# Recurrence scores in column tiles: blocks of 32 keys by 32 queries in place of whole 128 by 128 products

## The reference, cut to what matters

```python
def _hgrn2_scan(q, k, v, log_f, s0):
    """Chunkwise S_t = diag(f_t) S_{t-1} + k_t v_t^T, o_t = S_t^T q_t."""
    def step(S, xs):
        qc, kc, vc, lfc = xs
        b = jnp.cumsum(lfc, axis=1)
        b_last = b[:, -1]
        o_inter = jnp.einsum('bthk,bhkv->bthv', qc * jnp.exp(b), S)
        decay = jnp.exp(jnp.where(tri, b[:, :, None] - b[:, None, :], -jnp.inf))
        scores = jnp.einsum('bthk,btshk,bshk->bhts', qc, decay, kc)
        o_intra = jnp.einsum('bhts,bshv->bthv', scores, vc)
```

## Time and profile before

| what | value |
|---|---|
| runs, median (lowest to highest) | 2563.21 us (2562.05 to 2564.33), 3 runs |
| profiled execution, its own time | 2560.08 us |
| its span, first to last instruction | 2558.3 us |
| mean granted PE clock | 0.992 |
| PE busy | 2489.7 us (97%), 13364 matmul records |
| PEld busy | 1947.6 us (76%), 13364 weight loads |
| DVE busy | 1195.6 us (47%) |
| ACT busy | 604.2 us (24%) |
| POOL busy | 269.0 us (11%) |
| level scores, line 831, on PE | 120.5 us in 896 records |
| diagonal, line 828, on PE | 16.1 us in 128 records |
| DMA, mean over the span | 111 GB/s |

### The profile page before, as it was taken

One profiled execution on the slowest core, in us unless ns is written; L12 is line 12 of the kernel. 1 busy time (PEld: TensorE's weight loads), 2 busy tenths in 40 slices (PEclk: granted clock), 3 DMA queues, 4 the chain that ended last, 5 costly groups with the idle time before them and its releaser, 6 DMA issues.

```text
span 2558.3 us, 32946 instructions
## 1 busy us (share of the span) xinstructions
PE 2489.7 (97%) x13364; PEld 1947.6 (76%) x13364; DVE 1195.6 (47%) x2007; ACT 604.2 (24%) x1205; POOL 269.0 (11%) x194
## 2 busy tenths in 40 slices
PE   7999999999999898999999999999999999999999
PEld 3688888888887577867885444788885687889998
DVE  3176696696786613343234111256663014116961
ACT  3123233232332113143224000121211023113211
POOL 0011211122121000000000000112120000003410
PEclk9999999999999999999999999999999999999999
DMA  9443343443334042410520222233243132354662
GB/s 357 165 171 139 118 148 116 142 169 115 131 110 137 26 131 82 132 50 23 142 66 1 66 66 90 82 90 85 83 111 85 51 83 66 113 175 124 173 178 63
DMA packets 320673, 284.88 MB, mean 111 GB/s; under 512 B 27137, under 2 KB 300169, under 8 KB 320057
## 3 DMA queue, kind: packets, MB, share of 16 engines
q1 hardware_dynamic: 318810, 279.08, 35.4%
q0 software_dynamic: 1280, 4.20, 0.5%
q10 hardware_dynamic: 479, 0.13, 0.0%
HBM read 280.24 MB, written 3.15 MB: 111 GB/s over the span
## 4 chain that ended last, share of the span: by engine, by line
PE 79%; DVE 13%; issue 3%; ACT 2%; DMA 1%; SPq 0%; DVEq 0%; ACTq 0%
PE ps L1454 11%; PE ps L1383 10%; PE ps L733 7%; PE ps L1533 5%; PE ps L793 4%; PE ps L1521 4%; PE ps L1421 3%; PE ps L1395 3%; PE ps L784 2%; PE ps L917 2%; PE ps L935 2%; PE ps L1012 2%; PE ps L831 2%; DVE arena L2451 2%; DVE arena L2090 2%
## 5 line engine op out<-in xcount | busy, mean ns | idle before, releaser
L1383 PE MATMUL ps<-hT,ring_mem 128*128 128x512 f32 (+1 forms) x768 | 250.3, 486 | 0.0
L1383 PEld LDWEIGHTS ps<-hT,ring_mem 128*128 128x128 f32 x768 | 145.9, 190 | 101.3 <-issue 91.4
L2382 DVE TENSOR_TENSOR arena<-ps,arena 128x512 f32<-128x512 f32 (+1 forms) x48 | 26.8, 558 | 291.3 <-PE ps L1395 291.3
L733 PE MATMUL ps<-xT,ring_mem 128*128 128x256 f32 x672 | 159.8, 381 | 1.6 <-DVE ring_mem L2134 1.4
L733 PE MATMUL ps<-hT,ring_mem 128*128 128x256 f32 x672 | 158.8, 379 | 0.0
L733 PEld LDWEIGHTS ps<-xT,ring_mem 128*128 128x128 f32 x672 | 126.7, 190 | 22.8 <-issue 3.8
L733 PEld LDWEIGHTS ps<-hT,ring_mem 128*128 128x128 f32 x672 | 126.1, 190 | 18.9 <-issue 2.9
L1454 PE MATMUL ps<-hT,arena 128*128 128x256 f32 (+1 forms) x704 | 131.6, 331 | 6.9 <-ACT hT L512 6.9
L831 PE MATMUL ps<-arena,K_c 128*128 128x128 f32 x896 | 120.5, 289 | 11.8 <-ACT K_c L1717 11.7
L831 PEld LDWEIGHTS ps<-arena,K_c 128*128 128x128 f32 x896 | 116.9, 195 | 18.9 <-ACT K_c L1717 11.5
L1454 PE MATMUL ps<-arena 128*128 128x256 f32 (+1 forms) x704 | 129.6, 327 | 0.0
(11 more groups left out here) (316 smaller groups left out, 4302.5 us busy)
## 6 DMA issues: line engine op xcount, KB each, us to landing
ring_mem<-in_w_mod_dram SPq DMA_DIRECT2D x24, 2048.0 KB, 7.7
ring_mem<-in_w_up_dram SPq DMA_DIRECT2D x88, 512.0 KB, 5.2
ring_mem<-in_hg_w_in_dram SPq DMA_DIRECT2D x40, 1024.0 KB, 5.2
ring_mem<-in_w_in_dram SPq DMA_DIRECT2D x30, 1024.0 KB, 5.4
ring_mem<-in_w_down_dram SPq DMA_DIRECT2D x16, 1408.0 KB, 7.0
ring_mem<-in_ada_w_dram SPq DMA_DIRECT2D x8, 2048.0 KB, 7.7
ring_mem<-in_mla_w_in_dram SPq DMA_DIRECT2D x9, 1024.0 KB, 5.5
ring_mem<-in_hg_w_out_dram SPq DMA_DIRECT2D x8, 1024.0 KB, 12.2
```

The lines of the kernel that those rows point to most:

```text
L733: mm = PE.matmul(dst, left[:, k, :], right[:, k, :], start=k == 0, stop=k == 3)
L1383: mm = PE.matmul(ps[:, j, 0:n], wj[:, k, m * 128:m * 128 + 128], hT[:, k, c0:T], start=k == 0, stop=k == 7)
```

## The change

Each product of 128 keys by 128 queries is replaced by products over tiles on the diagonal of the unit, each with its own columns of the array and its own PSUM partitions. For the diagonal and levels 1 to 6 (h up to 32) a tile has 32 keys and 32 queries, four to a unit. For h below 32 the queries are those of the same 32 tokens; at h = 32 they are those of the neighbouring 32 (`c ^ h`), all from one direction's buffer. Level 7 (h = 64) takes two tiles of 64 keys by 64 queries. What else stands in the two banks is not written any more, and the masks do not select it. Nothing is changed on DVE, ACT, POOL or in the DMAs.

```diff
--- before.py
+++ after.py
@@ -819,16 +819,24 @@
                     pe.wait_ge(rt_ready, raised(i * 2))
             else:
                 pe.wait_ge(kc_ready, i * LEVELS + term)
+            h = 1 << term >> 1
+            w_ = 64 if h == 64 else 32
             for b in range(2):
                 if term:
                     pe.wait_ge(lv_free, i * 16 + 2 * term + b - 1)
                 for u in range(4 * b, 4 * b + 4):
-                    dst = ps[:, LV[b], (u % 4) * 128:(u % 4) * 128 + 128]
-                    if term == 0:
-                        mm = PE.matmul(dst, k_sum[:, u * 128:u * 128 + 128], q_st[:, u * 128:u * 128 + 128], start=True, stop=True)
-                    else:
-
-                        mm = PE.matmul(dst, K_c[:, u * 128:u * 128 + 128], comb(Qw, 1 << (term - 1), u), start=True, stop=True)
+                    for c in range(0, 128, w_):
+
+                        if term == 0:
+                            q0, queries = c, q_st[:, u * 128 + c:u * 128 + c + w_]
+                        elif h < w_:
+                            q0, queries = c, view(Qw, (2 * h, w_ // (2 * h)), (PC + h, 2), (1, h), at=u * 128 + c)
+                        else:
+                            q0 = c ^ h
+                            at_ = u * 128 + q0 + (PC if q0 & h else 0)
+                            queries = Qw[:, at_:at_ + w_]
+                        keys = (K_c if term else k_sum)[:, u * 128 + c:u * 128 + c + w_]
+                        mm = PE.matmul(ps[c:c + w_, LV[b], (u % 4) * 128 + q0:(u % 4) * 128 + q0 + w_], keys, queries, start=True, stop=True)
                 mm.then_inc(lv_full, 1)
 
         def hg_turn_tensor(pe, i):
```

## The result

The changed kernel takes **2576.31 us** in the median (2572.26 to 2578.66, 5 runs) beside 2563.21 (2560.6 to 2564.33, 5 runs) of the kernel before: a ratio of 1.0053 (95% interval 1.0038 to 1.0067), some 13 us slower. The forecast of 2546 had the wrong sign, and the result lies above its range.

The account below looks back on a forecast made before the run. Scores on PE bound the first turn; middle turns run mostly through DVE, and DVE waits for scores in the tail. Gains 7.5 + 9.6 + 3.6 less 4 for fetches are 16.7 us: 2546 us median, range 2537 to 2561.

Parts of the forecast that it names:

- the fetch at the returns: At the loop's five returns: fetching the longer body costs 0.8 us each, 4 us, mostly hidden behind the mean products.
- rival (4): Last recurrence: PE idles more, its clock falls for two more stretches, some 5 us longer, 2551 us; chance 0.05.
- rival (1): Loop returns: the body no longer stays in PE's instruction memory, 2.5 us a return, 2555 us, at the bound 2562; chance 0.18.
- A block: 0.75 us: One score term on PE, 128 instructions near 6 ns each: 0.75 us where it took 1.78.
- rivals (2) and (3): PE's blocks: narrow matmuls queue, 2554 us, chance 0.10; or instruction supply lags, 40 ns a pair, 2606 us, chance 0.12.
- Level 7: 1.2 us: Level 7's block in two tiles takes about 1.2 us instead of 1.88, giving 0.7 us a middle turn.
- First turn: 7.5: First turn of the loop: 8.1 us less on PE, all on the chain, of which 7.5 reach the end.
- Level 1: 0.9 a turn: Middle turns: faster level 1 scores give DVE its 0.69 us wait and the 0.21 ahead of line 2150.
- Levels 2 to 6: nothing, beside DVE's chain: Middle turns: levels 2 to 6 are off the chain; their 4 us become waits of PE and gain nothing.
- Last recurrence: 3.6: Last recurrence: DVE's three waits for scores, 1.94, 0.57 and 1.14 us, can all go, 3.6 us.
- PE's new idle time in a middle turn: PE newly idles ahead of levels 3 to 6 and line 733, ended by ACT's K_c and DVE's lines 2142 and 2191.
- the signs listed: Wrong if a block takes over 1.8 us, a middle turn over 99.9 us, or PE's clock in the turns is below 1.00.

Follow-up runs that it names:

- e1: The changed kernel with PE's six looped turns written out, so PE never branches back: 2543.23 us, ratio 0.9929 to the kernel before.
- e3: The changed kernel with levels 5 and 6 in whole products inside the loop, a body of 1834 instructions: 2574.4 us, ratio 1.0044.
- e4: The changed kernel with levels 4 to 6 in whole products inside the loop, a body of 1738 instructions: 2573.18 us, ratio 1.0041.
- e7: The kernel before, without tiles, line 733's products in the loop done in two halves of 128 columns, 1770 instructions: 2591.33 us, ratio 1.0116.
- e14: The changed kernel, levels 3 to 6 whole in the loop (1642 instructions), first looped turn written out with all but level 6 in tiles: 2565.05 us.
- e6: The changed kernel with levels 3 to 6 in whole products inside the loop, a body of 1642 instructions: 2545.85 us, ratio 0.994.
- e12: The changed kernel, levels 4 to 6 whole in the loop (1738 instructions), first looped turn written out ahead, in tiles throughout: 2543.86 us, ratio 0.9925.
- e5: The changed kernel, first looped turn written out, only levels 1 and 7 in tiles in the five remaining looped turns (1450 instructions): 2538.35 us.
- e9: The changed kernel with every turn written out for PE, levels 1 and 7 alone in tiles in turns 3 to 7: 2536.92 us, ratio 0.9904.
- e13: The changed kernel, levels 3 to 6 whole in the loop (1642 instructions), first looped turn written out, in tiles throughout: 2544.17 us, ratio 0.9931.
- e2: The kernel before, without tiles, its six looped turns written out for PE as a control: 2560.79 us, ratio 0.9993.

## Why the prediction was wrong

**The term that failed is the fetch at the returns**: "I take 0.8 us a return, 4 us, taking most of a fetch to lie behind the two mean products". Measured are 31 us for five returns by the turns of e1 and the changed kernel (523.3 − 492.5), 6.2 each; the rows of e3, e4, e7 and e14 have the same wait. Three things were off.

- What was priced as one transfer is more. The branch takes 4.2 to 4.5 us, over five times 0.8, and above even the upper bound of 3.9.
- Hardly any of it lies behind the mean products. They end 1.98 us after the start of the last group, and PE still stands for 3.55: of a branch of 4.25 us only some 0.7 is covered, since the sequencer comes to it while they run and no sooner.
- The clock falls in the gap. The first eight records lose 1.5 us by it, and where the stretch at 1.2 GHz is 6.8 us long instead of 3.4, the turn has 105.2 to 105.6 us instead of 104.1 to 104.2. e14 shows the share of it: without the fall a return costs 3.7 to 3.8 us. This was in rival (4) only for the last recurrence, never as what a wait of rival (1) would bring with it.

So rival (1) was the right mechanism, at 0.18, and its price of 2.5 us, bound 3.9, was too low: at 6.2 the prediction's own sum gives 2546 − 4 + 31 = 2573, 3 us from the result. The sentence from the Trainium skill ("Runtime: NRT & Kernel Launch", section "Instruction fetch mechanics") gives the 2048 instructions in blocks of 256, from which the prediction itself worked out that each return would miss. The page's own warning is of a branch out of a window of two blocks. Taken so, 1322 instructions would wait as well, and the runs decide against it: up to 1738 return in 0.2 us. A memory of 2048 instructions with one block being fetched leaves seven blocks, and with that reading e4, e6, e12 and e14 agree. I set that reading against a wish, that PE would have work queued, and no row stood for it.

**The rest, by its own steps.**

- *A block: 0.75 us.* 0.59 ahead of line 491 and 0.70 ahead of a product over the whole array. The timeline of the changed kernel in its first turn, as the earlier trace rows:

```profile
144.06 0.76 PE L839 MATMUL ps<-arena,K_c 128*32 128x32 f32 x64
144.65 1.93 PE L491 MATMUL ps<-ring_mem,sil_cols 128*32 128x256 f32 x32
146.52 1.99 PE L733 MATMUL ps<-xT,arena 128*128 128x256 f32 x8
```

  64 records in 0.59 us, 9 ns each, or 4.6 ns for an instruction with its weight load. This also settles rivals (2) and (3), at 25 and 40 ns for a pair. The trace does not agree with the 25 ns that the Trainium skill gives for up to 64 columns ("TensorE: Matmul & The Clock Gate", section "Back-to-back issue gap"), at least not for four column tiles.
- *Level 7: 1.2 us.* 1.08. Its 0.7 a turn was right (0.70).
- *First turn: 7.5.* 7.6 (97.5 to 89.9 us, from its first line 733 to the end of its means). PE's 8.1 did not all come through: ahead of level 1 PE now waits 0.52 us for DVE's copy.
- *Level 1: 0.9 a turn.* 1.46. The 0.69 and the 0.21 of the earlier trace rows went, and two things that I had not counted. The kernel before, then e5, from line 2090 to line 2141 of before:

```profile
328.87 1.34 DVE L2093 COPY_PREDICATED arena<-arena,ps 128x512 f32<-128x512 int32 x2
...
331.51 0.42 DVE L2139 TENSOR_TENSOR arena<-arena 128x256 f32<-128x256 f32 x1 [0.20 <-DVE arena L2095]
332.14 0.42 DVE L2141 TENSOR_TENSOR arena<-arena,ps 128x256 f32<-128x256 f32 x1 [0.20 <-PE ps L733]
```

```profile
315.47 2.22 DVE L2104 TENSOR_TENSOR arena<-arena 128x1024 f32<-128x1024 f32 x1
317.52 1.37 DVE L2107 COPY_PREDICATED arena<-arena,ps 128x512 f32<-128x512 int32 x2
...
320.19 0.43 DVE L2153 TENSOR_TENSOR arena<-arena 128x256 f32<-128x256 f32 x1 [0.20 <-DVE arena L2109]
320.53 0.41 DVE L2155 TENSOR_TENSOR arena<-arena,ps 128x256 f32<-128x256 f32 x1
```

  A second wait for line 733, ahead of line 2141, falls away too (0.63 us from start to start become 0.34), and line 2090, 2.25 us to the start of the next, takes 2.05.
- *Levels 2 to 6: nothing, beside DVE's chain.* Too good: nothing came off, and the eighth collision cost 0.94. So a middle turn without its return gained 1.22 and not 1.6: two errors that nearly cancel, 98.7 where 98.3 was forecast. What a faster engine triggers, POOL's step, was not asked. And the seventh turn was not like the others: it went from 98.73 to 98.53 us, 0.20 in place of 1.6. In e9, with levels 1 and 7 alone in tiles there too, it takes 97.48.
- *Last recurrence: 3.6.* 4.9. Of the three waits of the earlier trace rows those of 1.94 and 0.57 us are gone, and the one of 1.14, at level 7, is down to 0.57: 3.1 us. Another 0.95 came from the diagonal, which the prediction did not count: from the start of the means to the first line 2088, now 2096, it takes 9.17 us in place of 10.12. One of the instructions without a bracket, and that of level 7:

```profile
861.30 1.22 DVE L2098 TENSOR_TENSOR arena<-arena 128x1024 f32<-128x1024 f32 x1
...
876.17 1.23 DVE L2098 TENSOR_TENSOR arena<-arena 128x1024 f32<-128x1024 f32 x1 [0.57 <-PE ps L839]
```

- *PE's new idle time in a middle turn* stands where it was placed:

```profile
355.53 0.77 PE L839 MATMUL ps<-arena,K_c 128*32 128x32 f32 x64 [2.38 <-ACT K_c L1725]
...
360.33 1.99 PE L733 MATMUL ps<-xT,ring_mem 128*128 128x256 f32 x8 [1.18 <-DVE ring_mem L2142]
```

Of the signs listed, two came true: the middle turns are longer than 99.9 us, and PE's clock in them is 0.95 to 0.97.

## What to carry to other kernels

A change that adds instructions to a loop's body has a cost that no row of the kernel before shows: count the body before and after. By the rule that these runs allow, a body of up to 1537 instructions on PE stays in any place (1792 less the 255 by which it can begin in its block), one above 1792 in none, and between them the place decides. Give each return that waits 4 to 6 us, or write the loop out (e1), or put the new form only where it stands on the chain (e5: two terms of eight carry the whole gain of a middle turn, and the body stays short). A stall is to be priced with what follows it, here the clock. And where a chain runs through DVE, look at which side of a POOL instruction each of its steps starts: the faster PE turned one of them around and lost 1 us a turn.

## What was not expected of the hardware

- The body's place counts, not only its size: the same 1738 instructions wait at each return (e4) or not at all (e12), the same 1642 not (e13) or at each (e14). Adding or taking code ahead of a loop can so change its time by about 5 us a turn.
- A body that doesn't fit is fetched through in every turn, ten fetches each in the changed kernel, and only the fetch behind the branch costs: e1 makes 122 without a gap, and e2, with 100 in place of 75, takes no longer than before.
- Time at the lower clock costs only where PE is what others wait for: 3.4 us of it in e1's middle turns cost nothing that e6, without them, gains (98.70 and 98.64 us), while the same 3.4 us behind a return cost 1.5.
- The same gap of 3.4 to 3.6 us is followed by a lower clock at two of e14's returns and not at the other two. Which it will be, no run here tells.
